# Attention of an encoder step: both heads of a pair in one step, on halves of TensorE's array

## What is computed

```
def attend(q, k, v, bias, valid, sinks):
    s = einsum('bqhgd,bkhd->bhgqk', q, k) * (d ** -0.5) + bias
    ...
    if sinks is None:
        p = softmax(s, axis=-1)
    else:
        m = maximum(s.max(axis=-1), sk)
        p = exp(s - m[..., None])
        p = p / (p.sum(axis=-1, keepdims=True) + exp(sk - m)[..., None])
    o = einsum('bhgqk,bkhd->bqhgd', p, v)
```

## Time and profile before

| | |
|---|---|
| median of 3 runs | 3553.65 us |
| lowest and highest run | 3548.11 and 3559.67 us |
| span of the profiled execution, first to last instruction | 3540.5 us |
| TensorE busy | 3220.4 us (91% of the span) |
| TensorE weight loads, overlapping | 2904.5 us (82%) |
| VectorE, ScalarE, GpSimd busy | 1218.8, 1037.2, 155.4 us |
| mean granted TensorE clock | 0.922 of full speed |
| runs of stage A, of C's first seven pairs, of its last | 104 to 437, 1862 to 2480, 2480 to 2567 us of the span |

### The profile page before, as it was taken

How to read it: one execution, slowest core, us unless ns; L and a number is a source line. 1 busy time by engine, 2 the same in 40 slices (tenths; PEclk the granted TensorE clock), 3 DMA queues, 4 the chain that set the end, 5 groups by cost and what they waited for, 6 DMA issues and landing times.

```text
span 3540.5 us, 53095 instructions
## 1 busy us (share of the span) xinstructions
PE 3220.4 (91%) x18909; PEld 2904.5 (82%) x18909; DVE 1218.8 (34%) x2578; ACT 1037.2 (29%) x2090; POOL 155.4 (4%) x197
## 2 busy tenths in 40 slices
PE   6999988888679999999949999999994999999997
PEld 4655587787679999999948878788694999999996
DVE  3333333332442232323472222222227232323326
ACT  4322233333241111122243333333224212121123
POOL 2000000000100000000020000000002000000000
PEclk9999988877889999999969999999596999999998
DMA  9444212211101111111121111111020111111111
GB/s 307 134 138 135 89 34 26 26 19 69 36 24 38 51 42 51 45 39 57 36 75 47 41 38 38 38 38 38 13 85 12 42 47 43 52 33 56 48 33 64
DMA packets 279679, 201.65 MB, mean 57 GB/s; under 512 B 25932, under 2 KB 270356, under 8 KB 279156
## 3 DMA queue, kind: packets, MB, share of 16 engines
q1 hardware_dynamic: 271748, 166.31, 16.9%
q0 software_dynamic: 7792, 33.43, 2.8%
HBM read 181.49 MB, written 23.44 MB: 58 GB/s over the span
## 4 chain that ended last, share of the span: by engine, by line
PE 87%; DVE 6%; ACT 2%; issue 2%; DVEq 1%; DMA 1%; POOL 0%; SPq 0%; ACTq 0%; POOLq 0%
PE psum L679 22%; PE psum L680 21%; PE psum L681 21%; PE psum L824 6%; PE psum L770 5%; PE psum L850 5%; PE psum L838 3%; DVE x L1600 2%; DVE norm_buf L1557 1%; DVE diag L1548 1%; DVEq L1610 1%; ACT w_hi L1110 1%; PE psum L738 1%; PE psum L950 1%; PE psum L951 1%
## 5 line engine op out<-in xcount | busy, mean ns | idle before, releaser
L679 PE MATMUL psum<-h_hi,w_hi 128*128 128x352 f32 x3240 | 1081.4, 334 | 47.2 <-DVE w_lo L1496 19.1
L681 PE MATMUL psum<-h_hi,w_lo 128*128 128x352 f32 x3240 | 1053.0, 325 | 2.6 <-issue 2.6
L680 PE MATMUL psum<-h_lo,w_hi 128*128 128x352 f32 x3240 | 1053.4, 325 | 1.9 <-issue 1.9
L679 PEld LDWEIGHTS psum<-h_hi,w_hi 128*128 128x128 f32 x3240 | 620.0, 191 | 79.3 <-issue 31.0
L680 PEld LDWEIGHTS psum<-h_lo,w_hi 128*128 128x128 f32 x3240 | 621.6, 192 | 7.6 <-issue 7.6
L681 PEld LDWEIGHTS psum<-h_hi,w_lo 128*128 128x128 f32 x3240 | 619.3, 191 | 2.8 <-issue 2.8
L1496 DVE TENSOR_TENSOR w_lo<-w_raw,w_hi 128x1024 fp32r<-128x1024 f32 x231 | 282.2, 1224 | 698.1 <-ACT w_hi L1110 698.1
L679 PE MATMUL psum<-ff_hi,w_hi 128*128 128x352 f32 x1056 | 342.5, 324 | 3.9 <-DVE w_lo L1496 3.6
L1110 ACT ACTIVATE w_hi<-w_raw 128x1024 fp32r<-128x1024 f32 x231 | 242.5, 1053 | 353.6 <-PE psum L681 342.3
L680 PE MATMUL psum<-ff_lo,w_hi 128*128 128x352 f32 x1056 | 341.9, 324 | 0.0
L681 PE MATMUL psum<-ff_hi,w_lo 128*128 128x352 f32 x1056 | 341.9, 324 | 0.0
(11 more groups left out here) (307 smaller groups left out, 3547.3 us busy)
## 6 DMA issues: line engine op xcount, KB each, us to landing
ada_m<-in_w_ada SPq DMA_DIRECT2D x40, 1024.0 KB, 5.2
w_raw<-in_w_ffn_gate SPq DMA_DIRECT2D x88, 192.0 KB
w_raw<-in_w_ffn_up SPq DMA_DIRECT2D x88, 192.0 KB
w_raw<-in_w_ffn_down SPq DMA_DIRECT2D x112, 128.0 KB
w_raw<-in_w_in_c SPq DMA_DIRECT2D x48, 192.0 KB
x<-x_spill POOLq DMA_DIRECT2D x2, 4224.0 KB, 12.8
ada_s<-in_w_ada SPq DMA_DIRECT2D x8, 1024.0 KB, 11.3
w_raw<-in_w_ffn_down SPq DMA_DIRECT2D x128, 64.0 KB
```

Of the source, the lines that this page charges most:

```text
L679: nc.tensor.matmul(out, w_hi[:, slot, k], hi[:, k, c], start=(k == 0), stop=False)
L680: nc.tensor.matmul(out, w_hi[:, slot, k], lo[:, k, c], start=False, stop=False)
L681: last = nc.tensor.matmul(out, w_lo[:, slot, k], hi[:, k, c], start=False, stop=(k == kt - 1))
```

## The change

Both heads of a pair now go through one step together, nine steps in place of 18 and one more to drain.

- Scores: for each cut of the keys the matmul of head 0 (rows 0 to 63 of the array) is followed by that of head 1 (rows 64 to 127). Each head has its own two banks.
- Values: the value columns are now stationary (128 rows, 64 columns) and the transposed probabilities move; head 0 writes partitions 0 to 63 of the one output bank, head 1 partitions 64 to 127. The output comes out features on partitions, so `o_tok` and its transposes are gone, and `o_hi` and `o_lo` are written block by block.
- The division by the row sum moves ahead of the transposes: VectorE scales the probabilities of both heads in SBUF when both exponentials are done.
- In A the minimum and the sink are handled for both heads at once, with one more small subtraction and one exponential for both.
- TensorE's order in step i: scores of i, transposes of head 0 of i-1, fill, transposes of head 1, fill, values of i-1. In C both heads' transposes use the same banks; in A they have their own.
- ScalarE's order: copy of head 0 of i-1, exponential of head 0 of i, fill, exponential of head 1 of i, copy of head 1 of i-1, fill, `o_hi` of i-1.
- POOL's bias loads wait for the 17th and 18th minimum of a pair; its other waits are renumbered. A wait for the adaLN copies now stands ahead of each query projection in A, and the last adaLN transposes of a loop come behind the attention.
- Some buffers grow to hold both heads; later buffers shift by 384 bytes.

The core of the diff, TensorE first:

```
-        probs = scratch("probs", [128, 2, 640])
+        probs = scratch("probs", [128, 2, 2, 640])
-        o_tok = scratch("o_tok", [128, NBLK + 1, 128])
...
+        FILLS = {"A": [(1, 2)] * 10, "C": [(0, 1, 2)] + [(1, 2)] * 8 + [(0, 1, 2)]}
...
-                    pool.wait_ge(scores_read, hp * 18 + (CREDIT + 72 - 18 + 9 * (e + 1)))
+                    pool.wait_ge(scores_read, hp * 18 + (CREDIT + 72 - 18 + 17 + e))
...
+                def turned(n, e):
+                    m, first = qrows(n), c["slots"][e]
+                    pe.wait_ge(p_done, N(n) * 2 + (e + 1))
+                    pe.wait_ge(t_read, R(2 * n + (e if kind == "C" else 0)))
+                    for s, (_, kn) in enumerate(key_blocks(kind, n)):
+                        last = tr(tps[0:kn, first + s, 0:m], c["probs"][0:m, (n + par) % 2, e, 128 * s:128 * s + kn], ident[0:m, 0:m])
+                    last.then_inc(t_done, 1)
...
+                for i in range(10):
+                    if i < 9:
+                        pe.wait_ge(scores_read, N(i) * 2 + CREDIT)
+                        for s, (blk, kn) in enumerate(cuts):
+                            for e in range(2):
+                                rows = slice(64 * e, 64 * e + 64)
+                                last = nc.tensor.matmul(psum[0:m, score_bank(e) + col // 512, col % 512:col % 512 + kn],
+                                                        q[rows, 128 * i:128 * i + m], keys(blk, kn, rows, k, kct), start=True, stop=True)
...
+                    work(i, 0)
+                    if i:
+                        turned(i - 1, 0)
+                    work(i, 1)
+                    if i:
+                        turned(i - 1, 1)
+                    work(i, 2)
+                    if i:
+                        pe.wait_ge(t_read, R(2 * n + 2))
+                        pe.wait_ge(ol_done, one(N(n)))
+                        for s, (blk, kn) in enumerate(kb):
+                            for e in range(2):
+                                cols = slice(64 * e, 64 * e + 64)
...
+                                last = nc.tensor.matmul(oacc[cols, 0:m], v, probs_t[0:kn, e, s, 0:m],
+                                                        start=(s == 0), stop=(s == len(kb) - 1))
+                        last.then_inc(o_done, 1)
...
+                    pe.wait_ge(ada_copied, t * 10 + (8 + 2))
                     act_tile("qa", t, (plan["qa"][0] + par) % 2, h)
...
-                    pe.wait_ge(ol_done, one(t * 2))
```

ScalarE:

```
+                for i in range(10):
+                    work(i, 0)
+                    if i:
+                        copy(i - 1, 0)
+                    if i < 9:
+                        exps(i, 0)
+                    work(i, 1)
+                    if i < 9:
+                        exps(i, 1)
+                    if i:
+                        copy(i - 1, 1)
+                    work(i, 2)
+                    if i:
+                        act.wait_ge(o_done, N(n) + 1)
+                        A(tile_of(o_hi, it)[:, :, 128 * n:128 * n + m], oacc[:, 0:m].unsqueeze(1), ACT.Copy).then_inc(oh_done, 1)
```

VectorE, behind the two reductions of step i and `work(i, 0)`:

```
+                        dve.wait_ge(exp_done, N(i) * 2 + 2)
...
+                        V.reciprocal(rsum[0:m, b, :], total[0:m, b, :])
+                        dve.drain()
+                        for e in range(2):
+                            V.tensor_scalar(probs[0:m, b, e, 0:w], probs[0:m, b, e, 0:w], rsum[0:m, b, e:e + 1], None,
+                                            ALU.mult).then_inc(p_done, 1)
+                    work(i, 1)
+                    work(i, 2)
+                    if i:
+                        dve.wait_ge(oh_done, N(n) + 1)
+                        V.tensor_tensor(tile_of(o_lo, it)[:, :, cs], oacc[:, 0:m].unsqueeze(1), tile_of(o_hi, it)[:, :, cs].bitcast(F32),
+                                        ALU.subtract).then_inc(ol_done, 1)
```

More of the change, by code:

```diff
@@ L809, in attention, with work @@
                 c = KINDS[kind]
-                N = lambda n: it * 18 + (c["n0"] + n)
+                N = lambda n: it * 9 + (c["n0"] + n)
                 R = lambda n: it * (18 + c["pre"]) + (c["r0"] + c["pre"] + n)
-                lag, sb, f0 = c["lag"], c["score_bufs"], c["fill0"]
-                pre()
[L814 to L819, removed]
+                def work(i, spot):
+                    f = fills(kind, i, spot)
+                    if fill and f is not None:
+                        fill(f)
@@ L853, in attention @@
[L853 to L864, removed]
+                        for s, (blk, kn) in enumerate(cuts):
[3 more added lines that the diff above has]
+                                                        q[rows, 128 * i:128 * i + m], keys(blk, kn, rows, k, kct), start=True, stop=True)
+                                if s == len(cuts) - 1:
+                                    last.then_inc(scores, 1)
+                            col += kn
@@ L1082, in _ @@
             pair(7, 1, True)
-            pe.wait_ge(ol_done, one(24))
+            pe.wait_ge(ol_done, one(108))
             out_tiles(1)
@@ L1169, in copies, with attention @@
                 split_next(i + g0, slot)
-            def attention(kind, it, sinks, fill, pre):
+            def attention(kind, it, par, sinks, fill, pre):
                 c = KINDS[kind]
[L1173 to L1187, removed]
-                    p = n % 9
-                    m, kb = qrows(p), key_blocks(kind, p)
-                    act.wait_ge(t_done, TD(n) + 1)
@@ L1207, in attention @@
[L1207 to L1217 removed]
+                        A(probs_t[:, e, 0:full, 0:m], tps[:, first:first + full, 0:m], ACT.Copy)
@@ new lines, in copy, with work @@
+                        A(probs_t[0:TS, e, full, 0:m], tps[0:TS, first + full, 0:m], ACT.Copy).then_inc(t_read, 1)
+                def work(i, spot):
+                    f = fills(kind, i, spot)
+                    if fill and f is not None:
+                        fill(f)
+                pre()
+                for i in range(10):
[11 more added lines that the diff above has]
+                    if i:
+                        n, m = i - 1, qrows(i - 1)
+                        act.wait_ge(o_done, N(n) + 1)
+                        A(tile_of(o_hi, it)[:, :, 128 * n:128 * n + m], oacc[:, 0:m].unsqueeze(1), ACT.Copy).then_inc(oh_done, 1)
@@ new lines, in attention, with work @@
+                N = lambda n: it * 9 + (c["n0"] + n)
+                probs = c["probs"]
+                def work(i, spot):
+                    f = fills(kind, i, spot)
+                    if fill and f is not None:
+                        fill(f)
+                for i in range(10):
+                    if i < 9:
+                        m, (w, c0) = qrows(i), score_width(kind, i)
+                        b = (i + par) % 2
+                        mn = mins[0:m, b, :]
+                        for e in range(2):
+                            if i == 0:
+                                if kind == "A":
+                                    dve.wait_ge(bias_raw[e], it * 16 + 16)
+                                else:
+                                    dve.wait_ge(bias_ok[e], it + 1)
+                            dve.wait_ge(scores, N(i) * 2 + (e + 1))
+                            b_ = score_bank(e)
+                            sc = psum[0:m, b_:b_ + 2, :].rearrange("p b c -> p (b c)")[:, 0:w]
+                            apart(dve)
+                            op = V.tensor_tensor_reduce(out=probs[0:m, b, e, 0:w], in0=sc, in1=neg_bias[0:m, e, c0:c0 + w],
+                                                        scale=1.0, scalar=3.0e38, op0=ALU.add, op1=ALU.min, accum_out=mn[:, e:e + 1])
+                            if not sinks:
+                                op.then_inc(scores_read, 1)
@@ L1962, in fill @@
                         split_lo(hp * 3 + (3 + g0 + f // 3 + 2), (g0 + 3 * (1 - par) + f // 3) % 2)
-                attention("C", hp, False, None if last else fill)
+                attention("C", hp, par, False, None if last else fill)
             with dve.Fori(0, 3) as j:
```

186 lines of the change are left out of this document (67 added, 119 removed).

## The result

The changed kernel took 3355.78 us (median of 4 runs, 3331.57 to 3357.25), the kernel before beside it 3556.48 (3548.11 to 3559.67): a ratio of 0.9429 [0.9391, 0.9468], 201 us less. The forecast was 107 less and the range ended at 3390, so the direction was right and the size was not. By profiled executions the difference is 187.4 us (3540.5 less 3353.1).

A forecast was written before the change was run, and what follows sets the result against it. The prediction took TensorE, 87% of the chain of waits, as the bound. Savings of 63 us in seven mid pairs, 6 in the last pair and 38 in stage A made 107, so 3447 us; range 3390 to 3541.

The forecast's parts named there:

- the staircase: Scores and values on array halves: two products take three record times; 5.9 and 5.1 us less a pair; chance 0.50.
- the lower bound of the text: Scores of one mid pair in C: price with both halves always busy, 9.1 us against 18.2 before.
- the sample step: Last of a head's nine steps in C, 544 keys: scores put at 1.5 us, its values left unchanged.
- The rival of full halves: Scores and values: both array halves always busy, 37 us more gained, 3410 us in all; chance 0.15.
- The new wait: Before the values in C: TensorE waits for ScalarE's second copy, queued behind both next exponentials; 3.5 us a pair lost.
- The last pair: Last pair of C, carrying no next projection: runs at about half the rate, 6 us gained.
- Stage A: Sliding-window stage, four rounds: shorter scores and values 4.6 us, shorter tail 5 us, so 9.5 a round, 38 in all.
- The outputs' own transposes: After the values in C: nine block transposes and a wait of 0.43 us go, 1.5 us less a pair.
- The fixed part of the values: Group cost of values on column halves: put at 0.2 us; without it values come out 1.6 us a pair lower.
- Scaling the probabilities: VectorE in C: two passes of 640 columns, about 0.55 us each, costing TensorE nothing.
- POOL's late bias loads: Bias rows of the next pair, loaded after the last step: 11 us remain until needed, so no cost.
- The weight loads: Slower rival, scores and values on halves: loads no longer hidden, 168 us on top, 3615 us; chance 0.12.

## Why the prediction was wrong

**The step that failed: the staircase.** It said that "in program order head 0's second record runs beside head 1's first, so two products take three record times". The two halves take their records independently, as long as one need not pass more than three waiting ones of the other. Scores fell by 62.9 us in the seven pairs, 9.0 a pair, where 5.9 was put and 9.1 was the lower bound of the text; values by 49.9, 7.1 a pair, where 5.1 was put. Of that second miss of 2.0, 0.9 is the staircase (8.7 us put for the full blocks, 7.8 measured), 0.7 the sample step, which was left unchanged in the sum (1.58 us a pair before, 0.84 now), and 0.35 the old price of the full blocks, 14.15 and not 13.8. So the staircase is 28 us of the 80 that were missed, and the values' other two parts are 8. The rival of full halves was right on this step, and had 0.15; its 3410 was still 54 us too high, for the terms below. The row against it ("the records come head by head") was about the order in which records are issued; that it also is the order in which they start was assumed, and no row showed it.

The Trainium skill, "TensorE: Matmul & The Clock Gate", Part 3, had packed tiles run concurrently, by which the rival was near. The traces agree on this: against the same order without halves, scores shrink by 115.3/63.7 = 1.81 for two row halves, values by 108.8/60.2 = 1.81 for two column halves, their groups keeping a fixed part.

**The new wait: right in place, too large.** 3.5 us a pair was forecast. The values wait 0.84 a pair, three times, 0.5 at the longest, so the three short waits of 0.3 were right and the three longer ones (0.75, 0.75, 1.1) do not stand there. ScalarE's chain was as forecast: V begins at 2168.70, 4.26 us after the end of S, where the sum gave 4.0 and handoffs. But TensorE comes later than the 3.86 it was given, at 3.99. And part of the wait lies on another row: the next projection part waits for ScalarE's evacuation of the one bank, 13.9 us in place of 6.4. With the 5.1 us that stood before values anyway now gone, the idle ahead of projections and values grew from 18.2 to 26.6 us, 1.2 a pair and not 3.5: 16 us of the miss.

**The last pair: 6 forecast, 26 measured.** The text kept it at "about half the rate" throughout. By the estimate above, 16 of the 26 are what any pair loses, so the same halves and the same order, and 10 the clock.

**Stage A: 38 forecast, 50 measured with all four tails.** The tails were right: the outputs' transposes and their waits are gone, 13.7 us in the table and 7.0 behind the fourth round, where 20 was put. So was the direction of the scores and values, 33.5 us less where the staircase had 18. Against that stand 7.0 us more of waits ahead of transposes and projections, which were not in the sum. In 3.6 us of them transposes wait for VectorE's scaling (four times, 0.9 at the longest), which the prediction named as a sign of being wrong. And 5.6 us more of transposes stand against 5.9 less of projections. That last gain was not in the sum either: behind the tails of before, in which TensorE waits, the projection began at the lower clock, 0.29 us a record; behind three of the four short tails of now it begins at the higher, 0.16 a record. The first 3 us of such a projection, before and now:

```profile
190.98:194.00 3.02, 3.02 (x11) 3.02 (x11) 0.67 (x2) 0.52 (x1) 0.00 (x0) 0.50 0.02 5
```

```profile
181.20:184.20 3.00, 2.99 (x18) 2.99 (x19) 0.31 (x2) 0.14 (x1) 0.00 (x0) 1.00 0.80 254
```

**Right.** The outputs' own transposes (1.5 a pair; 1.6). The fixed part of the values, 0.2: it is 1.24 - 10 x 0.109 = 0.15. That it can't be zero was the rule of the Trainium skill, "TensorEngine Tiling (Array Packing)", Key Properties; the traces agree as far as before, on the whole array, the values' groups (0.26 us for 2 records, 1.16 for 10) leave only 0.04, but no run shows that a drain is the cause. Scaling the probabilities, 0.55 estimated, is 0.551 (L1688), and no transposes wait for it in the mid pairs (in A they do, as said). POOL's late bias loads cost nothing: no idle stands ahead of the scores in the mid pairs but one of 0.9 us, without a releaser. The weight loads did not come out of hiding: 379 us of them lie in the 487, and the halves overlap all the same.

## What to carry to other kernels

Two products of 64 rows, or of 64 columns, cost little more than one when they go to the two halves of the array and alternate closely in TensorE's order; measure one group from start to start to see which case it is, and expect a loss when one half has more than four records in a row (four cost up to 0.05 us here, six 0.24). When an engine's step shrinks, look at the order of the others next: moving one ScalarE copy ahead of an exponential gave 16 us more. And a stretch at the lower clock is no fixed price: price it at both levels, and look at whether work behind a long wait begins at the lower one.

## What was not expected of the hardware

Matmul records of one half start ahead of waiting records of the other, past up to three (0.71 us after the first of ten, where starts in order would be at 9 x 0.109 = 0.98 or later). Records on the two halves start 5 to 8 ns apart. A last pair with 20 us of added idle matmuls was 15 us shorter than without, its granted clock going from 0.50 to 1.00 partway.
